# Half units for the second attention's queries and keys, another order in the first down projection, four banks in the last branches

## The reference, cut to what matters

```
first_block:  h = rmsnorm(x) @ w_in            # index, q, k, v, recurrent and gate columns
              x = x + (gate_a*ya + gate_b*yb) @ w_out
              up = rmsnorm(x) @ w_up
              x = x + (gelu(conv(up[:, :3072])) * up[:, 3072:]) @ w_down       # the first down projection
              x = x + sigmoid(rmsnorm(x) @ w_ple_gate) * (p @ w_ple_proj)
second_block: x = x + 0.5 * ((silu(gate) * up) @ ffn1_w_out)
              q_a,k_a,v_a, q_b,k_b,v_b, gates = split(rmsnorm(x) @ w_mix_in)
              y_a = chunked band attention (8 heads of 64);  y_b = differential attention (4 heads of 2*64)
              merged = g_a*(y_a @ w_branch_a) + g_b*(y_b @ w_branch_b)         # the last branches
              x = x + merged @ w_o;  x = x + 0.5 * swiglu(rmsnorm(x));  return rmsnorm(x)
```

## Time and profile before

| what | value |
|---|---|
| median of 3 runs | 1052.1 us (1051.61 to 1052.1) |
| the profiled execution, its own time | 1051.96 us |
| its span in the profile | 1050.2 us |
| mean granted clock of TensorE | 0.998 of full speed |
| instructions | 18083 |
| busy share of DVE, ACT, POOL | 74%, 56%, 18% |
| moved from memory | 184.94 MB, 177 GB/s over the span |

### The profile page before, as it was taken

The page is one execution under the profiler, slowest core; times in us unless marked ns, Lnnn a source line. Parts: engine busy times, 40 slices in busy tenths (PEclk is TensorE's granted clock), DMA queues, the critical chain, the costliest instruction groups (busy, mean ns, idle before and its releaser), DMA issues.

```text
span 1050.2 us, 18083 instructions
## 1 busy us (share of the span) xinstructions
PE 1037.2 (99%) x6894; PEld 948.7 (90%) x6894; DVE 776.7 (74%) x962; ACT 588.9 (56%) x831; POOL 183.8 (18%) x209
## 2 busy tenths in 40 slices
PE   8999999999999999999999999999999999999998
PEld 7899999899888887899888888999989998888887
DVE  5799875768999996558887866575686688878653
ACT  5665799445656555457545444446576455454442
POOL 0400001222311211012222221010000222222210
PEclk9999999999999999999999999999999999999999
DMA  7745366755766666466776576664434557765761
GB/s 232 243 148 159 121 203 198 241 161 162 198 172 188 187 178 196 120 204 195 204 199 185 140 215 181 201 200 160 160 122 161 161 161 201 197 180 143 218 183 41
DMA packets 289762, 186.94 MB, mean 178 GB/s; under 512 B 6719, under 2 KB 286342, under 8 KB 289702
## 3 DMA queue, kind: packets, MB, share of 16 engines
q1 hardware_dynamic: 289006, 184.97, 59.9%
q10 hardware_dynamic: 696, 1.14, 0.3%
HBM read 184.94 MB, written 1.08 MB: 177 GB/s over the span
## 4 chain that ended last, share of the span: by engine, by line
PE 83%; DVE 10%; ACT 3%; issue 3%; DVEq 0%; DMA 0%; ACTq 0%; POOL 0%; POOLq 0%
PE psum L1886 19%; PE psum L1922 18%; PE psum L2391 10%; PE psum L1891 10%; PE psum L2394 5%; DVE wl L1260 5%; PE psum L2443 3%; PE psum L1861 2%; PE psum L1863 2%; PE psum L1862 2%; DVE logit L1693 2%; PE psum L2446 1%; DVE page_x L1664 1%; ACT logit L979 1%; DVE page_x L1676 1%
## 5 line engine op out<-in xcount | busy, mean ns | idle before, releaser
L1260 DVE TENSOR_TENSOR wl<-raw,wh 128x2048 fp32r<-128x2048 f32 (+3 forms) x210 | 414.0, 1988 | 95.1 <-ACT wh L591 94.8
L591 ACT ACTIVATE wh<-raw 128x2048 fp32r<-128x2048 f32 (+3 forms) x211 | 329.9, 1582 | 26.2 <-PE psum L1863 11.9
L1886 PE MATMUL psum<-parts,wh 128*128 128x512 f32 x1226 | 294.1, 391 | 0.0
L1886 PEld LDWEIGHTS psum<-parts,wh 128*128 128x128 f32 x1226 | 224.9, 188 | 43.8 <-DVE wl L1260 0.5
L1922 PE MATMUL psum<-parts,wh 128*128 128x256 f32 x1120 | 203.3, 285 | 1.9 <-issue 1.1
L1922 PEld LDWEIGHTS psum<-parts,wh 128*128 128x128 f32 x1120 | 173.9, 192 | 3.6 <-issue 2.1
L1891 PEld LDWEIGHTS psum<-parts,wl 128*128 128x128 f32 x1226 | 158.0, 191 | 6.5
L1891 PE MATMUL psum<-parts,wl 128*128 128x256 f32 x1226 | 160.0, 283 | 0.0
L1922 PE MATMUL psum<-parts,wl 128*128 128x256 f32 x560 | 156.0, 283 | 0.0
L2391 PE MATMUL psum<-parts,wh 128*128 128x512 f32 x476 | 121.0, 394 | 2.6 <-POOL parts L1200 2.6
L957 ACT ACTIVATE page_q<-psum 128x512 f32<-128x512 f32 x68 | 40.4, 594 | 125.2 <-PE psum L1891 125.0
(11 more groups left out here) (267 smaller groups left out, 1223.5 us busy)
## 6 DMA issues: line engine op xcount, KB each, us to landing
raw<-in_ffn_w_in SPq DMA_DIRECT2D x88, 512.0 KB
raw<-in_w_up SPq DMA_DIRECT2D x48, 512.0 KB
raw<-in_w_in SPq DMA_DIRECT2D x23, 1024.0 KB
raw<-in_w_mix_in SPq DMA_DIRECT2D x20, 1024.0 KB
raw<-in_ffn_w_out SPq DMA_DIRECT2D x32, 448.0 KB
raw<-in_w_down SPq DMA_DIRECT2D x24, 512.0 KB
raw<-in_ffn_w_out SPq DMA_DIRECT2D x16, 512.0 KB
raw<-in_w_attn_br SPq DMA_DIRECT2D x4, 1024.0 KB
```

Source lines behind the costliest of these rows:

```text
L591: act.activation(place(wh, u), place(raw, u), ACT.Copy).then_inc(rounded, 1)
L1260: dve.tensor_tensor(place(wl, u), place(raw, u), place(wh, u).bitcast(F32), ALU.subtract).then_inc(rest, 1)
L1886: mm(banks[base + s], wh[:, u % RING, w:w + P], both[:, t0 + k, :, :].rearrange("p h t -> p (h t)"), start=(k == 0), stop=False)
```

## The change

1. The start: all four loads of x are issued by SP; ScalarE rounds unit 2 between the squares of the two halves, and unit 3 before it copies the inverse root; VectorE splits unit 2 before the norm and copies x before it scales the index keys; the spreading of the inverse moves into pair(2). GpSimd makes two low tiles of the first norm instead of five.
2. The first down projection takes its pieces in the order of `DOWN_ORDER`; loads, products and the wait of VectorE's sum follow it. The other two keep their order. ScalarE's and VectorE's programs keep theirs.
3. e = 6 to 9 are made by `gate_unit`; halves are numbered 0 to 23; e = 10 and 11 and the branches get their banks explicitly; values (O) move from the odd to the even steps, ahead of the turning there.
4. The branches take four banks in turn.

```diff
-                           "PG", "KA", "VA", "QB", "KB", "VB", "GA'", "GB'")}
+                           "PG", "KA", "VA", "VB", "GA'", "GB'")}
+READER["QB"] = READER["KB"] = "-"
...
+DOWN_ORDER = {"DN1": [(0, 0), (0, 1), (1, 0), (1, 1), (0, 2), (1, 2)] + [(c, r) for c in range(2, 8) for r in range(3)]}
+for _name in ("DN2", "DN3"):
+    DOWN_ORDER[_name] = [(c, r) for c in range(8) for r in range(3)]
+def chunk_done(name, c):
+    return DOWN_ORDER[name].index((c, 2)) + 1
...
-POOL_LOWS = {0: 5, 2: 3, 4: 5}
-LATE_BEFORE = {0: 0, 2: 3, 4: 8}
+POOL_LOWS = {0: 2, 2: 3, 4: 5}
+LATE_BEFORE = {0: 0, 2: 6, 4: 11}
...
-for _e, _work in {6: dict(S=6), 8: dict(S=8, T=6), 9: dict(O=6), 10: dict(S=10, T=8), 11: dict(O=8), 12: dict(S=12, T=10),
-                  13: dict(O=10), 14: dict(S=14, T=12), 15: dict(O=12), 16: dict(S=16, T=13), 17: dict(O=13),
-                  18: dict(T=14), 19: dict(O=14)}.items():
+for _e, _work in {6: dict(S=6), 8: dict(S=8, T=6), 10: dict(S=10, T=8, O=6), 12: dict(S=12, T=10, O=8),
+                  14: dict(S=14, T=12, O=10), 16: dict(S=16, T=13, O=12), 18: dict(T=14, O=13), 19: dict(O=14)}.items():
...
             if g_qa <= g < group(U["WO2"]):
+                if g >= group(U["BA"]):
+                    return banks[(g - group(U["BA"])) % 4]
+                if g in (g_qa + 10, g_qa + 11):
+                    return banks[g - g_qa - 10]
                 return banks[(1, 2, 0)[(g - g_qa) % 3]]
...
+        def half_number(e, s):
+            return 2 * (e - 6 if e < 10 else e - 8) + s
         def gate_bank(h):
-            return banks[(1, 2, 0)[h % 3]]
+            return banks[(1, 2, 0)[h % 3] if h < 8 else (2, 0, 1)[(h - 8) % 3]]
...
             for h in range(2):
-                sp.dma_start(xtok[:, 0, h * 512:(h + 1) * 512], xin[:, 0, h * 512:(h + 1) * 512]).then_inc(x_loaded[h], 16)
+                for i in range(2):
+                    sp.dma_start(xtok[:, i, h * 512:(h + 1) * 512], xin[:, i, h * 512:(h + 1) * 512]).then_inc(x_loaded[h], 16)
...
             square_tokens(0)
+            round_unit(2)
             square_tokens(1)
             act.wait_ge(stat_done, 1)
             act.activation(rms[:, :], msq[:, 0, :], ACT.Sqrt, bias=eps[:, :], scale=1.0 / D).then_inc(root_done, 1)
-            round_unit(2)
+            round_unit(3)
             copy_inv(0)
-            round_unit(3)
...
+            rest_unit(2)
             dve.wait_ge(sq_done, 2)
             dve.tensor_tensor(msq[:, 0, :], msq[:, 0, :], msq[:, 1, :], ALU.add).then_inc(stat_done, 1)
             norm_inverse(0)
-            rest_unit(2)
+            for e in range(4):
+                copy_x(e)
...
-                    dve.wait_ge(mm_done, g + 3 * c + 3)
+                    dve.wait_ge(mm_done, g + chunk_done(name, c))
...
-                if e >= 12:
-                    for h in (2 * (e - 12), 2 * (e - 12) + 1):
+                if 6 <= e < 10 or e >= 12:
+                    for h in (half_number(e, 0), half_number(e, 1)):
+                        dst, main, low = gate_tile(h), gate_bank(h)[:, 0:T], gate_low(h)
...
                         dve.wait_ge(half_low, h + 1)
-                        dve.tensor_tensor(gate_tile(h), gate_bank(h)[:, 0:T], gate_low(h), ALU.add).then_inc(half_added, 1)
+                        dve.tensor_tensor(dst, main, low, ALU.add).then_inc(half_added, 1)
...
-                    pe.wait_ge(half_added, (15, 16, 14)[g - group(U["BA"])])
+                    pe.wait_ge(half_added, 22 + g - group(U["BA"]))
+                elif g in (group(U["QA"]) + 10, group(U["QA"]) + 11):
+                    pe.wait_ge(half_added, g - group(U["QA"]) - 4)
+                elif group(U["BA"]) + 3 <= g < group(U["WO2"]):
+                    if g > group(U["BA"]) + 3:
+                        pe.wait_ge(read_d, READ_BY["D"][g - 3])
...
+                for j, (c, r) in enumerate(DOWN_ORDER[name]):
+                    u, nk, k0 = u0 + j, pieces[r], sum(pieces[:r])
+                    ps, w0 = banks[down_base(name, c)], half(u) * SLOT // 2
+                    if r == 0:
+                        pe.wait_ge(read_d, READ_BY["D"][g0] + c - 2)
+                    unit_ready(u)
...
                     if h < 3:
-                        pe.wait_ge(read_a, READ_BY["A"][group(U["QA"]) + 9 + h + 1])
+                        pe.wait_ge(read_a, READ_BY["A"][group(U["QA"]) + 3 + h + 1])
+                    elif h in (9, 10):
+                        pe.wait_ge(read_a, READ_BY["A"][group(U["QA"]) + h + 1 + 1])
                     else:
-                        pe.wait_ge(half_added, h - 2)
+                        pe.wait_ge(half_added, 8 if h == 8 else h - 2)
...
-                elif e >= 12:
+                elif e >= 6:
                     gate_unit(e)
...
+                if "O" in MIX2[e]:
+                    values(MIX2[e]["O"])
                 if "T" in MIX2[e]:
                     for t in tiles_turned(MIX2[e]["T"]):
                         turn(t)
-                if "O" in MIX2[e]:
-                    values(MIX2[e]["O"])
```

More of the change, by code:

```diff
@@ L514, in load_down, with pieces @@
                 wv = A[w][0].rearrange("(k p) n -> p k n", p=P)
[L515 to L522, removed]
+                for j, (c, r) in enumerate(DOWN_ORDER[name]):
+                    def pieces(slot, k0=sum(parts[:r]), nk=parts[r]):
+                        return [(slot[:, 0:nk * P].rearrange("p (k n) -> p k n", k=nk),
+                                 wv[:, k0:k0 + nk, c * P:(c + 1) * P])]
+                    load(U[name] + j, pieces)
             load_up("UP1", "w_up", H1)
@@ L2137, in _ @@
             half_pair(1, 1, (0, 1), **raw_parts)
-            spread_inv(0)
             half_pair(1, 1, (2,), **raw_parts).then_inc(mm_done, 1)
-            pair(2, parts=unscaled(0))
+            pair(2, parts=unscaled(0), between=lambda: spread_inv(0))
             pe.wait_ge(x_copied, 4)
@@ L2372, in ffn_down @@
                 hidden = parts[:, HIDDEN["UP" + name[2]]:H1 + K, :, :]
-                def one(c):
-                    ps = banks[down_base(name, c)]
-                    pe.wait_ge(read_d, READ_BY["D"][g0] + c - 2)
-                    k0 = 0
-                    for r, nk in enumerate(pieces):
-                        u = u0 + 3 * c + r
-                        unit_ready(u)
-                        w0 = half(u) * SLOT // 2
-                        if c == 0 and r < 2:
-                            pe.wait_ge(lo_done, lows + k0 + nk)
-                        for k in range(nk) if c == 7 else ():
-                            first, last = k0 + k == 0, k0 + k == sum(pieces) - 1
-                            ins = three(ps[:, 0:T], u % RING, w0 + k * P, hidden[:, k0 + k, 0, :], hidden[:, k0 + k, 1, :], first, last)
-                        for ks in (range(nk),) if c < 7 else ():
-                            for k in ks:
-                                if c == 0 and r == 2:
-                                    pe.wait_ge(lo_done, lows + k0 + k + 1)
-                                mm(ps, wh[:, u % RING, w0 + k * P:w0 + k * P + P],
-                                   hidden[:, k0 + k, :, :].rearrange("p h t -> p (h t)"), start=(k0 + k == 0), stop=False)
-                            for k in ks:
-                                ins = mm(ps[:, 0:T], wl[:, u % RING, w0 + k * P:w0 + k * P + P], hidden[:, k0 + k, 0, :],
-                                         start=False, stop=(k0 + k == sum(pieces) - 1))
-                        ins.then_inc(mm_done, 1)
-                        k0 += nk
@@ L2398, in ffn_down @@
-                for c in range(8):
-                    one(c)
+                for j, (c, r) in enumerate(DOWN_ORDER[name]):
+                    u, nk, k0 = u0 + j, pieces[r], sum(pieces[:r])
[3 more added lines that the diff above has]
+                    unit_ready(u)
+                    if c == 0 and r < 2:
+                        pe.wait_ge(lo_done, lows + k0 + nk)
+                    if c == 7:
+                        for k in range(nk):
+                            ins = three(ps[:, 0:T], u % RING, w0 + k * P, hidden[:, k0 + k, 0, :], hidden[:, k0 + k, 1, :],
+                                        k0 + k == 0, k0 + k == sum(pieces) - 1)
+                    else:
+                        for k in range(nk):
+                            if c == 0 and r == 2:
+                                pe.wait_ge(lo_done, lows + k0 + k + 1)
+                            mm(ps, wh[:, u % RING, w0 + k * P:w0 + k * P + P],
+                               hidden[:, k0 + k, :, :].rearrange("p h t -> p (h t)"), start=(k0 + k == 0), stop=False)
+                        for k in range(nk):
+                            ins = mm(ps[:, 0:T], wl[:, u % RING, w0 + k * P:w0 + k * P + P], hidden[:, k0 + k, 0, :],
+                                     start=False, stop=(k0 + k == sum(pieces) - 1))
+                    ins.then_inc(mm_done, 1)
```

38 lines of the change are left out of this document (15 added, 23 removed).

## The result

The changed kernel takes 1054.09 us, the median of 19 runs (1051.76 to 1054.84), against 1051.61 us of the kernel before (19 runs, 1049.94 to 1053.26). The ratio is 1.002, with a 95% interval of 1.0014 to 1.0027: 1.5 to 2.8 us slower. That lies across the bound of 0.2% between "same" and "slower". The forecast was 1053.2, in a range of 1048.0 to 1055.5.

A forecast was written before the change was run, and what follows sets the result against it. TensorE, busy 99% of the span, was taken as the bound. Start -1.5, first down projection +1.6, attention +1.0 and banks 0 made +1.1 us on 1052.1, so 1053.2 us, range 1048.0 to 1055.5.

The forecast's parts named there:

- Start: Start of the kernel, up to pair(5): TensorE gets 1.5 us ahead; bounds -2.6 and 0.
- The wait at pair(5): Start: TensorE's 1.07 us idle before pair(5), put to GpSimd's low parts of the norm, goes whole.
- Dots(0): Start: held behind VectorE's scaled queries and unit 4's split, it keeps 0.45 of the 1.5 us gained at pair(2).
- First down projection: New piece order: two waits for low parts become one for a split, another follows, clock falls; +1.6 us, bounds -4.5, +1.9.
- Both waits: First down projection: 3.6 us for the fourth unit's split, then one at the seventh piece behind VectorE's late column 0 sum.
- one fall: First down projection: TensorE's clock drops from 2.4 to 1.2 GHz for 3.4 us behind an idle, costing 1.5 us.
- Attention: Second attention: -0.6 from wider products, new waits of 0.85 and 0.8 for VectorE's sums; +1.0 us, bounds -1.0, +2.6.
- Four banks: Last branches: the only wait, 0.5 us, is for low parts, not a bank, and stays; 0, bounds -0.5, +0.1.
- A: First down projection: ScalarE rounds the fourth unit sooner, so the new order hides the wait; 1047.1 us, chance 0.15.
- B: Attention and clock: no new waits in the attention and no fall of the clock; 1050.1 us, chance 0.15.
- C: Attention: its two small waits take the clock down, 1.5 us each; 1056.2 us, chance 0.07.
- D: Start: it keeps nothing, as what follows waits for VectorE or unit 4's load; 1054.7 us, chance 0.08.

The follow-up runs named there:

- start alone: Kernel before with only the edits of the start, including two GpSimd low tiles instead of five; 1050.31 us, ratio 0.9981.
- halves alone: Kernel before with only the half units (e = 6 to 9 by gate_unit), the moved values and the four banks; 1052.81 us, ratio 1.0016.
- order alone: Kernel before with only the new order of the first down projection (DOWN_ORDER and what follows it); 1053.92 us, ratio 1.0017.
- kept busy: Changed kernel with 28 unused products of 256 columns ahead of the first down projection's fourth piece; 1051.61 us, ratio 0.9999.
- sums first: Changed kernel with VectorE making the half sums ahead of the split at e = 7, 9, 13, 15 and 17; 1051.38 us, ratio 0.9999.
- Early split: Changed kernel with the first down projection's fourth unit rounded before ScalarE's last activation and split before VectorE's last product; 1047.96 us, ratio 0.9966.
- after, old order: Changed kernel with the first down projection's pieces in their old order; 1051.72 us, ratio 1.0.
- the twin of both repairs: The kernel of both repairs measured once more, beside its version with the old order of the first down projection; 1046.26 us, ratio 0.9944.
- both repairs: Changed kernel with the fourth unit split early and the half sums ahead of the splits; 1045.71 us, ratio 0.9945.

## Why the prediction was right, and where it was off

The added waits and the gains came where the prediction placed them, and for its reasons; the number came close in part by luck. Against the kernel before, +1.1 us was forecast and +2.1 measured by the ratio (+2.5 by the medians). The base of 1052.1 was the median of three runs, 0.5 us above that of 19, and the start gave 0.6 us more than forecast; both hid part of what the down projection cost.

**Start, -1.5 forecast, -2.1 measured** (-2.09 in the trace, -2.0 alone). The wait at pair(5) went, as said. Three steps were off. Pair(2) came 1.16 sooner, not 1.5, as ScalarE waited 0.56 us for unit 2's load. Dots(0) kept 0.94, not 0.45: unit 4's load was taken to be 0.15 late behind two more issues, and was early: SP issues it at 19.82 instead of 20.18, and ScalarE has it at 26.95 instead of 27.78. SP's wait for the first split absorbs the two issues whole (the next load goes out at 12.12, before at 12.25), and when SP issues it scatters between executions: 20.16 in start alone, 19.70 and 20.55 in two kernels with the old start. With the issue at 20.16 ScalarE still has the unit at 27.34, 0.44 sooner than before; why, no run tells. And GpSimd's two low tiles were to be done at 37.8, and took until 41.3. The 1.74 us per tile was a mean of two kinds. The durations of GpSimd's tiles (min/median/max, ns), before and after:

```profile
L1152 POOL TENSOR_TENSOR parts<-page_y,parts x5: 726/743/3855, 34.3 to 42.3; 128x256 fp32r<-128x256 f32 x5
```

```profile
L1159 POOL TENSOR_TENSOR parts<-page_y,parts x2: 3004/3932/4860, 33.5 to 38.3; 128x256 fp32r<-128x256 f32 x2
```

A tile takes 0.73 us by itself, and 3.0 and 4.9 beside VectorE's work here. GpSimd was done 0.7 us ahead of pair(5), not 4. What the 1.07 us of before were stays open, too: GpSimd was done at 43.00, when TensorE's scores ended, and pair(5) began 1.08 later. In halves alone and order alone it began 1.08 and 1.00 behind GpSimd's end, in start alone 0.44. That the wait went with the new start is shown, but not what it consisted of.

**First down projection, +1.6 forecast, 2.8 to 3.2 measured in the median run** (2.1 to 2.5 in all, less -2.1 and +1.4 for the other two). Both waits came where they were placed: 3.66 us at the fourth piece (forecast 3.6), 1.10 at the seventh. The second was forecast at 0.95 (408.25 less 407.3), for the reason that the trace shows: the splits start 2.32 behind the sum (402.78 to 405.10). By stretches it is +1.07 with no fall on either side (637.79 against 636.72), +1.7 to +2.1 with one on both (639.42 against 637.31 and 637.68), against a forecast of 1.6; and some 1.6 more in the 12 of 19 runs with a second half-rate stretch. The mis-sized term is the clock. I priced one fall at 1.5 on both sides, where before pays 0.6 to 1.0 for it and after 1.6, and the one wait of 3.7 us brings 6.8 us at half rate instead of 3.4 in most runs of the changed kernel. Only the profile of order alone shows the 6.8 us directly, and most of its timed runs have room for one stretch; for the changed kernel's runs it is inferred from their mean clock and times, and from kept busy, where it is gone.

**Attention, +1.0 forecast, +1.4 measured.** The waits are 0.85 and 0.84 us, forecast 0.85 and 0.8, at the places named and for the reason named (sums first removes both). What I left out is that a wait also costs a restart: the eight products behind 724.51 take 1.95 us to the start of the next group, where those behind 720.87 take 1.84. Taking both waits away gave 2.28 us, not 1.69: two restarts of 0.11 belong to it, and at e = 16 and 18, where nothing was forecast, waits of 0.06 and 0.07 and a restart of 0.11 and 0.14 behind them. Products, moved values and banks together gave 0.87, where the forecast had 0.6 for the products and 0 for the rest.

**Four banks, 0.** The wait for L1502 is still 0.49. Not tried by itself.

**The rivals.** A (1047.1) was wrong for its own condition: ScalarE doesn't get to the fourth unit sooner. Early split, which makes it so, gave 1047.96. B is not it, the waits are there. C: the waits in the attention took no clock down in any profile, nor in the runs of kept busy, which has both. D: the start kept all it gained.

## What to carry to other kernels

Reordering the consumer pays only when the units it now wants first are also made first on the engines that prepare them: follow the new order through every engine's program before judging it. When a half-unit's sum frees a bank, put it ahead of the next split in that engine's queue. And price an idle of TensorE not by its length alone: add the restart and what the clock does behind it, in most runs rather than in the one profiled (2.5 us of the median behind the 3.7 us here). Where the idle can't be avoided, products that nobody reads can fill it; they took those 2.5 us away.

## What the runs showed of the hardware

- The clock behind one and the same wait of 3.7 us was at half rate not at all (after, profiled), for 3.4 us (sums first) or for 6.8 us (order alone). Length alone doesn't tell what falls: a single wait of 1.25 us ahead of pair(5) was followed by 3.4 us at half rate in order alone, and one of 1.07 at the same place in before by none. Around two close together the clock fell in before and start alone, and did not in halves alone and "after, old order" (2.6 to 2.7 us in all four). Waits of 1.3 us and less at the fourth and seventh piece, in the attention and in the last branches were followed by none in any profile. 3.4 us at half rate cost 1.6 us of time.
- The mean granted clock also counts time without work for TensorE: up to 0.0014 of it was lost behind the last product, in "after, old order" and the twin of both repairs, at no cost.
- When GpSimd and VectorE both subtract one tile of SBUF from another, one of them stands. The second GpSimd tile after began at 38.32 and ended at 41.32, 0.6 us behind VectorE's split of 38.46 to 40.73, which ran at its usual 2.3 us. In both repairs GpSimd's L1210 began first (392.63, 0.74 us), and VectorE's split took 1.79 instead of 1.17. The Trainium skill, "SBUF — State Buffer", section "SBUF: two separate sides", calls the port pair that the two share an exclusive lock, held for the whole instruction by whichever starts first. The rows of both repairs agree (1.17 and what was left of the 0.74 make 1.88, measured 1.79). In those of after one instruction stands for the other too, but it is GpSimd, whose record begins 0.14 us ahead of the split's: which of the two gets the ports can't be told from the starts of the records.
